# Broadcast rows of the state-space and delta-rule stages: transposes of copied columns instead of products with a triangle

## The chip, the cores and the metric

The kernel runs on 1 core of one Trainium2 chip. The metric is the time of one execution on the device, in microseconds (us); the time given is the median of 3 runs. From the same kernel one profiled execution was taken, and all rows below are from it.

## The reference, cut to what matters

The program is a network of four layers on 512 tokens of width 1024: two layers with a mixer of three branches (attention, spatial gating, a Mamba-2 state space) and two with a gated delta rule, each between feed-forward parts. The change touches two places in it. Both need, for a head, the running sum `cs` of a log decay over the tokens, once as a column (a token on each partition) and once as a row spread over all 128 partitions, to form the decay between token `i` and token `j`:

```python
def segsum(a):                       # state space: a = A * dt, all 4 heads
    cs = jnp.cumsum(a, axis=-1)
    return jnp.where(tril, cs[..., :, None] - cs[..., None, :], -jnp.inf)

# delta rule: chunks of 64 tokens, 4 heads
g = jnp.cumsum(g.reshape(Bsz, N, C, H).transpose(0, 3, 1, 2), axis=-1)
decay = jnp.exp(jnp.where(causal, g[..., :, None] - g[..., None, :], -jnp.inf))
qk = jnp.einsum('bhncd,bhnmd->bhncm', q, k) * decay
q_dec = q * jnp.exp(g)[..., None]
```

The rest of those layers is projections, softmax, normalisations and the recurrences over chunks, which the change leaves as they are.

## The kernel before

T = 512 tokens are TT = 4 tiles of P = 128. The program is a chain of stages; in each, five engines (TensorE, VectorE, ScalarE, GpSimd, SyncE for the DMA queue) run lists of instructions that were written out by hand, in the order in which they stand in the code. Nothing reorders them: an engine that waits for a semaphore holds up all that stands behind it on that engine. A stage ends in a barrier of all engines. `M.ps` is the whole of PSUM, 8 banks of 512 fp32 columns; `M.ident` is the identity, `M.tri` the triangle of ones and `M.ones` a tile of ones.

**mixer1_rest** (twice, for the two layers of the first kind: it starts at 685.9 us and at 1805.0 us) does the state space, the spatial gating and the compressed attention. TensorE begins with `sums_col()`: `A.a` (tokens by tiles and heads) times the triangle gives all 16 running-sum columns in bank 2. Then follow `compress(0)` (32 matmuls, L1696), `turn_ws()` (L1794), `rows(0)`, `turn_x()` (L1801), `rows(1)`, `spatial(0)` and `spatial(1)` (L1770), `states(0, 0)` (L1715), `turn_local(0)` (L1780), `compress(1)`, `turn_local(1)`, `turn_hidden()` (L1807), and later `scores(0)` (L1739), `rows(2)`, `states(0, 2)`, `scores(1)`, `rows(3)`, `turn(0)` (L1750). `rows(h)` makes the spread row of head `h` in bank 4 or 5 (L1704): for each of 4 tiles `j` a matmul whose stationary side is the column `A.a[:, j, h]` spread over 128 columns and whose moving side is the triangle followed by ones, 512, 384, 256 and 128 columns wide, added up in one bank. ScalarE's `decays(g, k)` (L1886, L1887, L1890) reads these banks, with the columns `cs` and `ncs` = -`cs` as bias.

VectorE begins this stage with a memset (L2091), `statistics()` of the spatial gating's layer norm (L2030 to L2033), `bias_columns()` (L2040), then `sums_copy()` (L2044, L2045), which copies the sums from bank 2 to `cs` and `ncs`, then `ws_mask()` (L2049, waits for `turn_ws`), a reciprocal (L2097), four `center(i)` (L2025, L2026, two instructions each), whose last signals `v_normed`, for which `spatial(0)` waits; after them `steps_times_x` (L2055), `gate` (L2016), `low_local(0)` (L170), `weigh(0, 0)` (L1965, L1967), `pre()` (L2060, waits for `compress(1)`; ScalarE then makes `cmp_x`, and `turn_hidden` waits for that). ScalarE begins with a Gelu (L1914), waits for `statistics()`, takes a root (L1916), then six Silu (L1918), one more (L1919), then `decays(0, 0)`.

**mixer2_delta** (twice: from 2413.6 us and from 3121.7 us) does the delta rule. TensorE makes the sums of `A.g` (L2521, L2522) in bank 7. Then for each of 4 token tiles `i`: the spread rows of the 4 heads (L2528, stationary `g` column spread, moving the 128-wide triangle), the rows of beta (L2534, transposes of a spread column), products `kk` (L2536) and `qk` (L2541), transposes of `k` and `v` (L2546, L2551) and `dense(i)`: 24 products of a projection that is done in between (L163 to L165). Before the rows of a tile `i` >= 1 it waits until VectorE has read the previous ones (`S.diff`). After the 4 tiles follow 28 rounds of the triangular inverse (`first_product` L2566 and L2568, `updates` L2577, `turn_inverse` L2586).

VectorE begins this stage with `low(0)` and `low(1)`, the low halves of two weight tiles (L170), each after a cast by ScalarE (L2658); behind them it copies the sums to `A.G` (L2811) and `A.gain` (L2812 to L2814). ScalarE's part in a tile is the Exp of the rows (L2710), the Exp of the differences (L2712), and behind that `evacuate(i)` of the product `dense(i)` (L2673) and the cast of the next weight tile (L2658), which stand ahead of L2710 of the next tile. VectorE's part is L2820, L2821 (differences from the rows), the low halves of the next weights, L2827 to L2842, and in the last tile the first masks of the inverse (`mask`, L2801 and L2805).

Of the kernel before, what the change touches and what calls it, by code (L numbers as in the profile page):

```python
# [22 lines left out]
P = 128  # L23
T = 512
TT = T // P
# [1621 lines left out]
def mixer1_rest(nc, M, A, I, l, mine, ahead):  # L1647
# [7 lines left out]
    with ExitStack() as memory, stage(  # L1655
# [34 lines left out]
        def _(pe):  # L1690
# [9 lines left out]
            def rows(h):  # L1700
                if h >= hpg:
                    pe.wait_ge(S.decay, hpg * TT)
                for j in range(TT):
                    mm = pe.matmul(M.ps[:, 4 + h % 2, j * P:T], A.a[:, j, h:h + 1].to_broadcast([P, P]), tri[:, 0:T - j * P],  # L1704
                                   start=(j == 0), stop=(j == TT - 1), skip_group_check=True)
                mm.then_inc(S.rows, 1)

            def states(g, k):
# [248 lines left out]
        def _(dve):  # L1957
# [131 lines left out]
                low_part(dve, M.h_low[:, n_ssd + g, :], xbc[:, g, :], M.h_high[:, n_ssd + g, :])  # L2089

            dve.memset(bias_c[:], MASKED).then_inc(S.bias_init, 1)  # L2091
            statistics()
            bias_columns()
            sums_copy()
            ws_mask()
            dve.wait_ge(S.root_ready, 1)
            link(dve.reciprocal(rstd[:], rstd[:]))  # L2097
# [360 lines left out]
def mixer2_delta(nc, M, A, I, l, mine, ahead):  # L2458
# [4 lines left out]
    UNITS = TT * LEVELS  # L2463
    sequence = [e for c in range(SCT) for e in ([3 * c, 3 * c + 1, 3 * c + 2] + ([GATED + c - 1] if c else []))] + [GATED + SCT - 1]
    place = {e: n for n, e in enumerate(sequence)}
    with ExitStack() as memory, stage(nc, f"delta_{l}", "sums chain gains gain_exp g_rows diff decay rows_exp q_scaled kk qk "
               "lt_ready qk_ready k_turned v_turned nat_ready masked t1 t1_copied x_up xy_ready y_turned x_copied u_ready w_ready u_copied w_copied "
               "ws state_read v_new o o_squared o_copied o_normed s_add s_ready root_ready prep_free mix_turned mix_high mix_ready sc_high "
               "w_high w_split product act_evacuated dve_evacuated gated squared sc_root sc_scaled pad gate_chain row_high", mine) as (block, S):
# [33 lines left out]
        def _(pe):  # L2503
# [19 lines left out]
            for i in range(TT):  # L2523

                if i >= 1:
                    pe.wait_ge(S.diff, i)
                for h in range(DH):
                    mm = pe.matmul(head(M.ps[:, 0], h), g_all[:, DH * i + h:DH * i + h + 1].to_broadcast([P, P]), tri,  # L2528
                                   start=True, stop=True)
                mm.then_inc(S.g_rows, 1)  # L2530
                if i >= 1:
                    pe.wait_ge(S.lt_ready, i)
                for h in range(DH):
                    pe.transpose(head(M.ps[:, 1], h), beta_all[:, DH * i + h:DH * i + h + 1].to_broadcast([P, P]), M.ident[:])  # L2534
                for h in range(DH):
                    mm = pe.matmul(head(M.ps[:, 2], h), tok(k, h, i), tok(k, h, i), start=True, stop=True)  # L2536
                mm.then_inc(S.kk, 1)
                if i >= 1:
                    pe.wait_ge(S.qk_ready, i)
                for h in range(DH):  # L2540
                    mm = pe.matmul(head(M.ps[:, 3], h), tok(k, h, i), tok(q, h, i), start=True, stop=True)  # L2541
                mm.then_inc(S.qk, 1)
                if i >= 1:
                    pe.wait_ge(S.nat_ready, i)
                for h in range(DH):
                    mm = pe.transpose(head(M.ps[:, 4], h), tok(k, h, i), M.ident[:])  # L2546
                mm.then_inc(S.k_turned, 1)
                if i >= 1:
                    pe.wait_ge(S.prep_free, i)
                for h in range(DH):  # L2550
                    mm = pe.transpose(head(M.ps[:, 5], h), tok(v, h, i), M.ident[:])  # L2551
                mm.then_inc(S.v_turned, 1)
                dense(i)
# [197 lines left out]
        def _(dve):  # L2751
# [56 lines left out]
            gate_link(dve.memset(A.prod[:, :, 0:SCCONV - 1], 0.0))  # L2808
            low(1)
            dve.wait_ge(S.sums, 1)  # L2810
            link(dve.tensor_copy(A.G[:], M.ps[:, 7, 0:16]))  # L2811
            link(dve.tensor_copy(A.gain[:, 0:16], M.ps[:, 7, 0:16]))  # L2812
            link(dve.tensor_tensor(A.gain[:, 16:32], M.ps[:, 7, 16:32], A.G[:], ALU.subtract))
            dve.tensor_copy(A.gain[:, 32:48], M.ps[:, 7, 16:32]).then_inc(S.gains, 1)  # L2814
            dve.wait_ge(S.gain_exp, 1)
# [220 lines left out]
```

## Time and profile before

| | |
|---|---|
| median of 3 runs | 3725.05 us (3722.63 to 3726.55) |
| span of the profiled execution, first to last instruction | 3722.3 us |
| median less that span | 2.7 us |
| TensorE matmul busy | 3579.8 us (96% of the span) |
| VectorE, ScalarE, GpSimd busy | 1981.1, 1221.2, 149.4 us |
| mean granted TensorE clock | 0.979 of full speed |

The profiled execution's own time is its span; what a timed run counts beyond that (launch and end) shows only as the 2.7 us between span and median. PE is TensorE's matmuls, PEld its weight loads, which run ahead under the matmul before; DVE is VectorE, ACT ScalarE. A matmul's duration in the trace contains its modelled way through the array, so two neighbours overlap, and PE looks busy across small waits. How long a group of matmuls holds TensorE is therefore read from the start of its first weight load to the start of the next group's. An fp32 matmul stands as two records, a transpose as one. PEclk is the granted clock: 1.00 is 2.4 GHz and 0.50 is 1.2 GHz.

### The profile page before, as it was taken

The numbers are of one execution on the slowest core, as the hardware profiler recorded it, in microseconds if no ns is written. First come the engines' busy times: TensorE is split into PE (matmuls) and PEld (weight loads), VectorE is DVE, ScalarE is ACT, GpSimd is POOL, SyncE is SP. The second block draws the span as 40 slices with busy tenths as digits, with TensorE's granted clock in tenths as the row PEclk, the third lists the DMA queues.
The fourth block names the chain that finished last, engine by engine and source line by source line (L and its number), as shares of the span: only waits on it lengthen the run. The fifth ranks groups of instructions, "written<-read, shape, count | busy, mean of one in ns | idle before, by whom it ended". The sixth has DMA issues, their size and how long they took to land. (4 is left out here: it accounts for less than half of the span.)

```text
span 3722.3 us, 43542 instructions
## 1 busy us (share of the span) xinstructions
PE 3579.8 (96%) x17858; PEld 2957.7 (79%) x17858; DVE 1981.1 (53%) x3057; ACT 1221.2 (33%) x1920; POOL 149.4 (4%) x212
## 2 busy tenths in 40 slices
PE   6999999999999999999999998999999999999999
PEld 4888778678887888777678886788788878878887
DVE  5555566666456755566663355665322366553233
ACT  2222334432223222334532233634222355342222
POOL 1110100001000110100000001000000000000000
PEclk8999999999999999999999999999999999999999
DMA  6664331145443654331133342211233312113332
GB/s 238 224 200 138 77 94 46 52 132 200 143 136 96 212 173 139 76 97 46 52 122 121 99 145 52 75 39 52 80 102 119 102 47 74 40 52 102 91 107 79
DMA packets 438042, 397.75 MB, mean 107 GB/s; under 512 B 53779, under 2 KB 390275, under 8 KB 437844
## 3 DMA queue, kind: packets, MB, share of 16 engines
q1 hardware_dynamic: 413028, 310.53, 27.5%
q0 software_dynamic: 24816, 84.45, 6.7%
q8 instruction: 141, 2.31, 0.3%
q14 instruction: 57, 0.47, 0.0%
HBM read 390.14 MB, written 4.78 MB: 106 GB/s over the span
## 5 line engine op out<-in xcount | busy, mean ns | idle before, releaser
L163 PE MATMUL m_ps<-m_h_high,ffn_w_high 128*128 128x512 f32 x2100 | 824.1, 392 | 0.8 <-DVE ffn_w_low L170 0.8
L164 PE MATMUL m_ps<-m_h_low,ffn_w_high 128*128 128x512 f32 x2100 | 819.4, 390 | 0.0
L165 PE MATMUL m_ps<-m_h_high,ffn_w_low 128*128 128x512 f32 x2100 | 819.3, 390 | 0.0
L165 PEld LDWEIGHTS m_ps<-m_h_high,ffn_w_low 128*128 128x128 f32 x2100 | 395.5, 188 | 83.7
L163 PEld LDWEIGHTS m_ps<-m_h_high,ffn_w_high 128*128 128x128 f32 x2100 | 396.0, 189 | 83.0 <-issue 0.8
L164 PEld LDWEIGHTS m_ps<-m_h_low,ffn_w_high 128*128 128x128 f32 x2100 | 396.1, 189 | 81.8
L953 ACT ACTIVATE ffn_sil<-m_ps 128x512 f32<-128x512 f32 x132 | 79.0, 599 | 1140.0 <-PE m_ps L165 1140.0
L163 PE MATMUL m_ps<-ffn_w_high,ffn_hid_high 128*128 128x512 f32 x1056 | 411.7, 390 | 0.0
L165 PE MATMUL m_ps<-ffn_w_high,ffn_hid_low 128*128 128x512 f32 x1056 | 411.0, 389 | 0.0
L164 PE MATMUL m_ps<-ffn_w_low,ffn_hid_high 128*128 128x512 f32 x1056 | 410.9, 389 | 0.0
L993 DVE TENSOR_TENSOR ffn_hid<-ffn_sil,m_ps 128x512 f32<-128x512 f32 x110 | 75.5, 687 | 561.3 <-ACT ffn_sil L953 561.3
L170 DVE TENSOR_TENSOR ffn_w_low<-m_raw,ffn_w_high 128x2048 fp32r<-128x2048 f32 (+1 forms) x168 | 303.6, 1822 | 111.6 <-ACT ffn_w_high L947 107.8
L170 DVE TENSOR_TENSOR ffn_w_low<-ffn_rows,ffn_w_high 128x1024 fp32r<-128x1024 f32 x132 | 161.5, 1224 | 292.1 <-ACT ffn_hid_high L961 291.8
L541 ACT CAST ffn_w_high<-ffn_rows 128x1024 fp32r<-128x1024 f32 x132 | 138.5, 1050 | 407.9 <-PE m_ps L165 395.4
L947 ACT CAST ffn_w_high<-m_raw 128x2048 fp32r<-128x2048 f32 x126 | 239.4, 1900 | 0.0
L165 PEld LDWEIGHTS m_ps<-ffn_w_high,ffn_hid_low 128*128 128x128 f32 x1056 | 198.2, 188 | 41.3
L163 PEld LDWEIGHTS m_ps<-ffn_w_high,ffn_hid_high 128*128 128x128 f32 x1056 | 198.2, 188 | 40.9
L164 PEld LDWEIGHTS m_ps<-ffn_w_low,ffn_hid_high 128*128 128x128 f32 x1056 | 198.2, 188 | 40.8
L381 DVE SCALAR_TENSOR_TENSOR ffn_ada_part<-ffn_rows,m_ccol,ffn_ada_part 128x512 f32<-128x512 f32 x224 | 168.1, 751 | 88.2 <-DMA ffn_rows<-in_ada_w 80.1
L367 POOL DMA_DIRECT2D ffn_rows<-in_ada_w x128 | 90.9, 711 | 1533.4 <-issue 939.1
L1490 ACT ACTIVATE attn_probs<-attn_probs,attn_shift 128x128 f32<-128x128 f32 (+3 forms) x128 | 71.0, 555 | 193.6 <-DVE attn_shift L1545 193.6
L163 PE MATMUL m_ps<-m_h_high,proj_w_high 128*128 128x512 f32 (+2 forms) x312 | 130.9, 420 | 1.8 <-DVE proj_w_low L170 1.8
(479 smaller groups left out, 5564.0 us busy)
## 6 DMA issues: line engine op xcount, KB each, us to landing
m_raw<-in_ffn_w SPq DMA_DIRECT2D x176, 512.0 KB, 4.7
ffn_rows<-in_ada_w POOLq DMA_DIRECT2D x128, 512.0 KB, 5.0
ffn_rows<-in_ffn_w SPq DMA_DIRECT2D x88, 512.0 KB, 3.5
m_raw<-in_w_in SPq DMA_DIRECT2D x32, 1024.0 KB, 5.3
m_raw<-in_ffn_w_gate SPq DMA_DIRECT2D x44, 512.0 KB, 3.8
m_raw<-in_ffn_w_up SPq DMA_DIRECT2D x44, 512.0 KB, 4.8
ffn_rows<-in_ffn_w_down SPq DMA_DIRECT2D x44, 512.0 KB, 3.3
m_raw<-in_w_out SPq DMA_DIRECT2D x24, 512.0 KB, 4.6
```

The source lines that it names most:

```text
L163: pe.matmul(out, sh, mh, start=first, stop=False, skip_group_check=True)
L164: pe.matmul(out, sh, ml, start=False, stop=False, skip_group_check=True)
L165: return pe.matmul(out, sl, mh, start=False, stop=last, skip_group_check=True)
L170: return dve.tensor_tensor(low, value, high.bitcast(F32), ALU.subtract)
L367: queue.dma_start(self.slots[:, n % 2], src).then_inc([S.ada0_landed, S.ada1_landed][n % 2], 16)
L381: dve.scalar_tensor_tensor(out=part, in0=self.slots[:, n % 2, j, :], scalar=self.M.ccol[:, k + j:k + j + 1], in1=part, op0=ALU.mult, op1=A ...
L541: return act.copy(self.high[f % self.SLOTS], self.raw[f % self.raws])
L947: act.copy(w_high[:, f % 2], M.raw[:, f % 2]).then_inc(S.wide_high, 1)
L953: act.activation(sil[:, f % 2, :], M.ps[:, 2 * (f % 2), :], ACT.Silu).then_inc(S.silu_done, 1)
L993: dve.tensor_tensor(hid[:, f, :], sil[:, f % 2, :], M.ps[:, 2 * (f % 2) + 1, :], ALU.mult).then_inc(S.hidden_done, 1)
L1490: ins = act.activation(probs(m, g), probs(m, g), ACT.Exp, bias=shift[:, m % 4, g:g + 1], accum_out=sums[:, p % 4, g, b:b + 1])
```

## The change

In `mixer1_rest`, `rows(h)` no longer multiplies by the triangle. It transposes, for each tile, the copied running-sum column `cs` spread over 128 columns, 128 columns wide, 4 in all. The first two heads now wait for the copy (`S.col_copied`), and VectorE's `sums_copy()` stands ahead of `statistics()`. In `mixer2_delta` the 4 rows of a tile are transposes of the copied columns `A.G`; the first tile waits for a new semaphore `g_copied`, which the copy to `A.G` signals, and VectorE waits for it itself before it reads `A.G`.

```diff
--- before.py
+++ after.py
@@ -1700,9 +1700,10 @@
             def rows(h):
                 if h >= hpg:
                     pe.wait_ge(S.decay, hpg * TT)
-                for j in range(TT):
-                    mm = pe.matmul(M.ps[:, 4 + h % 2, j * P:T], A.a[:, j, h:h + 1].to_broadcast([P, P]), tri[:, 0:T - j * P],
-                                   start=(j == 0), stop=(j == TT - 1), skip_group_check=True)
+                else:
+                    pe.wait_ge(S.col_copied, 1)
+                for i in range(TT):
+                    mm = pe.transpose(M.ps[:, 4 + h % 2, tokens(i)], cs[:, SH * i + h:SH * i + h + 1].to_broadcast([P, P]), M.ident[:])
                 mm.then_inc(S.rows, 1)
 
             def states(g, k):
@@ -2089,9 +2090,9 @@
                 low_part(dve, M.h_low[:, n_ssd + g, :], xbc[:, g, :], M.h_high[:, n_ssd + g, :])
 
             dve.memset(bias_c[:], MASKED).then_inc(S.bias_init, 1)
+            sums_copy()
             statistics()
             bias_columns()
-            sums_copy()
             ws_mask()
             dve.wait_ge(S.root_ready, 1)
             link(dve.reciprocal(rstd[:], rstd[:]))
@@ -2463,7 +2464,7 @@
     UNITS = TT * LEVELS
     sequence = [e for c in range(SCT) for e in ([3 * c, 3 * c + 1, 3 * c + 2] + ([GATED + c - 1] if c else []))] + [GATED + SCT - 1]
     place = {e: n for n, e in enumerate(sequence)}
-    with ExitStack() as memory, stage(nc, f"delta_{l}", "sums chain gains gain_exp g_rows diff decay rows_exp q_scaled kk qk "
+    with ExitStack() as memory, stage(nc, f"delta_{l}", "sums chain g_copied gains gain_exp g_rows diff decay rows_exp q_scaled kk qk "
                "lt_ready qk_ready k_turned v_turned nat_ready masked t1 t1_copied x_up xy_ready y_turned x_copied u_ready w_ready u_copied w_copied "
                "ws state_read v_new o o_squared o_copied o_normed s_add s_ready root_ready prep_free mix_turned mix_high mix_ready sc_high "
                "w_high w_split product act_evacuated dve_evacuated gated squared sc_root sc_scaled pad gate_chain row_high", mine) as (block, S):
@@ -2524,9 +2525,10 @@
 
                 if i >= 1:
                     pe.wait_ge(S.diff, i)
+                else:
+                    pe.wait_ge(S.g_copied, 1)
                 for h in range(DH):
-                    mm = pe.matmul(head(M.ps[:, 0], h), g_all[:, DH * i + h:DH * i + h + 1].to_broadcast([P, P]), tri,
-                                   start=True, stop=True)
+                    mm = pe.transpose(head(M.ps[:, 0], h), A.G[:, DH * i + h:DH * i + h + 1].to_broadcast([P, P]), M.ident[:])
                 mm.then_inc(S.g_rows, 1)
                 if i >= 1:
                     pe.wait_ge(S.lt_ready, i)
@@ -2808,8 +2810,9 @@
             gate_link(dve.memset(A.prod[:, :, 0:SCCONV - 1], 0.0))
             low(1)
             dve.wait_ge(S.sums, 1)
-            link(dve.tensor_copy(A.G[:], M.ps[:, 7, 0:16]))
+            dve.tensor_copy(A.G[:], M.ps[:, 7, 0:16]).then_inc(S.g_copied, 1)
             link(dve.tensor_copy(A.gain[:, 0:16], M.ps[:, 7, 0:16]))
+            dve.wait_ge(S.g_copied, 1)
             link(dve.tensor_tensor(A.gain[:, 16:32], M.ps[:, 7, 16:32], A.G[:], ALU.subtract))
             dve.tensor_copy(A.gain[:, 32:48], M.ps[:, 7, 16:32]).then_inc(S.gains, 1)
             dve.wait_ge(S.gain_exp, 1)
```

How the instructions stand now, at the three places where an engine waits or is waited for. First TensorE in `mixer1_rest`, from `turn_ws` on, before (`m_tri` moving with `a_a` stationary are the old rows):

```order
L1794 MATMUL m_ps<-m_ident,a_ws 128x128 x4
L1704 MATMUL m_ps<-m_tri,a_a 128x512
L1704 MATMUL m_ps<-m_tri,a_a 128x384
L1704 MATMUL m_ps<-m_tri,a_a 128x256
L1704 MATMUL m_ps<-m_tri,a_a 128x128
L1801 MATMUL m_ps<-m_ident,a_raw 128x128 x8
```

and the same stretch, to `states(0, 0)`, with the change (`rest_cs` is the copied column; `rows` is now L1706):

```order
L1795 MATMUL m_ps<-m_ident,a_ws 128x128 x4
L1706 MATMUL m_ps<-m_ident,rest_cs 128x128 x4
L1802 MATMUL m_ps<-m_ident,a_raw 128x128 x8
L1706 MATMUL m_ps<-m_ident,rest_cs 128x128 x4
L1771 MATMUL m_ps<-a_uv,rest_wsT 128x256 x4
L1716 MATMUL m_ps<-a_raw 128x512
```

Four matmuls of 1280 columns in all have become four transposes of 512 columns in all, at the same place. Next VectorE at the start of that stage with the change (before, the two rows of `rest_cs` and `rest_ncs` stood just ahead of `rest_wsT`):

```order
L2092 MEMSET rest_bias_c 128x992
L2045 COPY rest_cs<-m_ps 128x16
L2046 TENSOR_SCALAR rest_ncs<-m_ps 128x16
L2031 BN_STATS rest_stats<-a_uv 128x6 x4
L2033 BN_AGGR rest_mv<-rest_stats 128x2 x4
L2034 TENSOR_SCALAR rest_rstd<-rest_mv 128x4
```

The copy, with its wait for `sums_col`, now stands ahead of the statistics, for which ScalarE waits. Last, TensorE at the start of `mixer2_delta` with the change:

```order
L2522 MATMUL m_ps<-b_g,m_tri 128x16
L2523 MATMUL m_ps<-b_g,m_ones 128x16
L2531 MATMUL m_ps<-m_ident,b_G 128x128 x4
L2536 MATMUL m_ps<-m_ident,b_beta 128x128 x4
L2538 MATMUL m_ps<-b_qkv 128x128 x4
```

and VectorE at the same start:

```order
L170 TENSOR_TENSOR delta_w_low<-m_raw,delta_w_high 128x1024
L2810 MEMSET b_prod 128x2x2
L170 TENSOR_TENSOR delta_w_low<-m_raw,delta_w_high 128x1024
L2813 COPY b_G<-m_ps 128x16
L2814 COPY b_gain<-m_ps 128x16
L2816 TENSOR_TENSOR b_gain<-m_ps,b_G 128x16
```

No instruction has moved in this stage: but L2531 on TensorE, which stood third and waited for nothing of VectorE's, now waits for L2813, which stands behind both L170.

## Rows read from the trace of the kernel before

**Rows 1.** Timeline of the weight loads, first mixer1_rest: start, duration, instruction, idle time before.

```profile
694.15 0.30 PEld L1704 LDWEIGHTS m_ps<-m_tri,a_a 128*128 128x128 f32 x2
...
696.31 0.91 PEld L1801 LDWEIGHTS m_ps<-m_ident,a_raw 128*128 128x128 f32 x8
697.18 0.30 PEld L1704 LDWEIGHTS m_ps<-m_tri,a_a 128*128 128x128 f32 x2
...
699.34 1.60 PEld L1770 LDWEIGHTS m_ps<-a_uv,rest_wsT 128*128 128x128 f32 x8
...
706.17 0.42 PEld L1780 LDWEIGHTS m_ps<-m_ident,a_uv 128*128 128x128 f32 x4 [0.39 <-issue]
```

**Rows 2.** Timeline of VectorE in the same stretch.

```profile
694.46 0.69 DVE L2049 TENSOR_TENSOR rest_wsT<-m_ps,m_tri 128x512 f32<-128x512 f32 x1 [3.23 <-PE m_ps L1794]
...
698.54 0.48 DVE L2026 SCALAR_TENSOR_TENSOR a_uv<-a_uv,rest_rstd,a_ln_b 128x256 f32<-128x256 f32 x1
...
706.53 0.42 DVE L2060 TENSOR_TENSOR rest_cmp_x<-m_ps,a_cmp_b 128x256 f32<-128x256 f32 x1
```

**Rows 3.** Timeline at the starts of both mixer1_rest stages.

```profile
686.15 1.42 PE L1788 MATMUL m_ps<-a_a,m_ones 128*128 128x12 f32 x6
686.95 1.75 DVE L2030 BATCH_NORM_STATS2 rest_stats<-a_uv 128x6 f32<-128x256 f32 x4
...
1805.21 1.01 PE L1788 MATMUL m_ps<-a_a,m_ones 128*128 128x12 f32 x6
1806.04 1.75 DVE L2030 BATCH_NORM_STATS2 rest_stats<-a_uv 128x6 f32<-128x256 f32 x4
```

**Rows 4.** Timeline of ScalarE: its waits for the rows, first stage, then second.

```profile
696.66 1.28 ACT L1886 ACT_TABLE_LOAD   x1 [0.61 <-PE m_ps L1704]
...
699.65 0.58 ACT L1886 ACTIVATE rest_decay<-m_ps,rest_ncs 128x384 f32<-128x384 f32 x1 [0.86 <-PE m_ps L1704]
...
1817.18 0.58 ACT L1886 ACTIVATE rest_decay<-m_ps,rest_ncs 128x384 f32<-128x384 f32 x1
```

**Rows 5.** Timeline around rows(2), rows(3) and turn(0), first stage.

```profile
714.29 0.42 DVE L1990 TENSOR_TENSOR rest_score_c<-rest_score_c,rest_denom_c 128x248 f32<-128x248 f32 x1
...
717.45 0.88 PEld L1750 LDWEIGHTS m_ps<-m_ident,rest_score_c 128*31 128x31 f32 x8
```

**Rows 6.** Timeline of the weight loads at the start of the first mixer2_delta.

```profile
2413.59 0.30 PEld L2521 LDWEIGHTS m_ps<-b_g,m_tri 128*128 128x128 f32 x2 [1.36 <-issue]
...
2414.03 0.97 PEld L2528 LDWEIGHTS m_ps<-m_tri,b_g 128*128 128x128 f32 x8
...
2414.92 0.47 PEld L2534 LDWEIGHTS m_ps<-m_ident,b_beta 128*128 128x128 f32 x4
2415.36 0.97 PEld L2536 LDWEIGHTS m_ps<-b_qkv 128*128 128x128 f32 x8
...
2418.02 0.19 PEld L163 LDWEIGHTS m_ps<-m_h_high,delta_w_high 128*128 128x128 f32 x1
```

**Rows 7.** Timeline of VectorE there: the copy to A.G.

```profile
2417.10 0.17 DVE L2811 COPY b_G<-m_ps 128x16 f32<-128x16 f32 x1
```

**Rows 8.** Timeline of ScalarE and VectorE in and behind the last tile, first mixer2_delta.

```profile
2443.24 1.05 ACT L2658 CAST delta_w_high<-m_raw 128x1024 fp32r<-128x1024 f32 x1
2444.18 0.60 ACT L2710 ACTIVATE b_rows<-m_ps 128x512 f32<-128x512 f32 x1
...
2444.81 0.69 DVE L2820 TENSOR_TENSOR b_D<-m_ps,b_G 128x512 f32<-128x512 f32 x1 [2.44 <-ACT b_rows L2710]
...
2467.29 0.68 DVE L2801 TENSOR_TENSOR b_D<-b_LT,m_levels 128x512 f32<-128x512 f32 x1
```

**Rows 9.** Windows: stretch, its length, busy time by engine, PEclk, DMA share, GB/s.

```profile
682.70:686.10 3.40, 1.57 (x15) 1.46 (x15) 2.02 (x11) 1.29 (x3) 0.00 (x0) 1.00 0.02 5
686.10:692.90 6.80, 6.80 (x34) 4.51 (x35) 4.68 (x16) 5.19 (x7) 0.00 (x0) 0.50 0.00 0
...
1805.70:1809.10 3.40, 3.40 (x17) 2.15 (x19) 3.09 (x12) 1.82 (x3) 0.00 (x0) 0.50 0.00 0
```

## The prediction, as it stands on record

> **What bounds the kernel now.** I read the timeline of TensorE's weight loads first, from the start of one group to the start of the next, because the modelled ends of matmuls hide its waits; then what VectorE and ScalarE do in the same stretches; then the granted clock in windows. The reader is to see that TensorE is nearly always at work and the other engines mostly wait for it, but that this does not hold where the change is made. In `mixer1_rest` VectorE ends its last `center` at 698.54 + 0.48 = 699.02 us [rows 2], and TensorE begins `spatial(0)`, which waits for that, at 699.34 [rows 1]: 0.3 us apart, so two engines arrive together. At the start of `mixer2_delta` TensorE works from 2413.59 on without a gap [rows 6], and the copy to `A.G` is made only at 2417.10 [rows 7], since it is behind two casts' low parts; so far nobody waits for it but ScalarE. And both stages begin with a pause at the barrier, after which the clock can be at half.
>
> **The change part by part.**
>
> *The price of rows.* Old `rows(h)`: 696.31 - 694.15 = 2.16 us. Eight transposes of the same width took 697.18 - 696.31 = 0.87 us, 0.109 each [rows 1]; four transposes of a spread column, just what the new rows are, 2415.36 - 2414.92 = 0.44 us against 2414.92 - 2414.03 = 0.89 for the four products of a delta tile [rows 6]. So a `rows(h)` gives back 1.72 us and a delta tile 0.45. By count TensorE loses 8 x 1.72 + 8 x 0.45 = 17.4 us of work; what follows is how much of it ends up on the path. The lower end of the new price is this 0.44, the upper that of the products of equal width, 0.89.
>
> The Trainium skill, page "TensorE: Matmul & The Clock Gate", section "Part 4: PE-mode transpose", puts a full transpose at about 275 ns inside a kernel. This trace shows 109 ns, so it does not agree; by the page's figure the 64 transposes would cost an estimated 64 x 0.166 = 10.6 us more than by the row.
>
> *First half of mixer1_rest (rows(0), rows(1)).* `turn_ws` is not moved, and the copy is long there, so the new wait costs nothing. TensorE is through with both rows 2 x 1.72 = 3.44 us earlier, at 695.90. But `ws_mask` starts behind `turn_ws` at 694.46 and `center` ends at 699.02 whatever TensorE does [rows 2]: `spatial(0)` starts at 699.06 in place of 699.34. TensorE stands 3.16 us. From there to `turn_local(1)` it needs 706.17 - 699.34 = 6.83 us [rows 1], to 705.9, and VectorE's `pre()` was at 706.53 [rows 2], on ScalarE's chain. ScalarE waited 0.61 + 0.86 = 1.47 us for the rows in the first stage and not at all in the second [rows 4]. Against it stands the moved copy: VectorE now waits for the sums, which end at 686.15 + 1.42 = 687.57, then copies (some 0.3 us), so the statistics start at 687.9 in place of 686.95, 0.95 later; in the second stage 1805.21 + 1.01 + 0.34 = 1806.56 in place of 1806.04, 0.5 later [rows 3]. ScalarE's Silu and decays are queued behind them. Net at `turn_hidden`: 0.5 us gained in the first stage, 0.5 lost in the second, 0 in sum, if the clock holds.
>
> *The clock in that pause.* With TensorE busy 1.57 us of 3.40, the granted clock fell from 1.00 to 0.50, and stayed for 6.8 us in the first stage and 3.4 us in the second [rows 9]. That is 2.4 to 1.2 GHz. The new pause is 3.16 us with only transposes ahead of it. I expect one half-clock stretch of 3.4 us behind it, 1.7 us of work lost: TensorE is then at 699.06 + 6.83 + 1.7 = 707.6, 1.1 behind the old `pre()`. Ends: 0 and 1.1 + 1.7 = 2.8 per stage. The same page's section "Why this matters for your kernels" warns of idle gaps between bursts, after which the clock is back at half; by that rule, the trace agrees (0.50 behind the pause).
>
> *Second half (rows(2), rows(3)).* 3.44 us less work, but `turn(0)` waits for L1990, which ends at 714.29 + 0.42 = 714.71, and TensorE, 3.44 before 717.45, would be there at 714.01 [rows 5]. Gain 717.45 - 714.75 = 2.7; VectorE's chain behind (the next probabilities and `weigh(0, 3)`) takes, as I choose, 0.3 of it: 2.4. TensorE has less dense work here too, so another half-clock stretch is about as likely as not; it would cost 1.5, I count 0.7. Per stage 1.1 - 2.4 + 0.7 = -0.6, both -1.2 us.
>
> *Start of mixer2_delta.* The rows of tile 0 now wait for `A.G`: 2417.10 + 0.17 = 2417.27 [rows 7], TensorE goes on at 2417.31, 3.28 us after 2414.03. All that is queued behind waits too: beta's rows, `kk`, `qk`, two transposes, `dense(0)`. The latter came 2418.02 - 2414.92 = 3.10 us after the old rows' end; now 2417.31 + 0.44 + 3.10 = 2420.85, which is 2.83 late [rows 6]. ScalarE's evacuation and its cast of the next weights wait for `dense(0)`, so nothing absorbs it. Tiles 1 and 2 give back 0.45 each: 1.93 late at the end of `dense(2)`. Tile 3's 0.45 does not count: ScalarE does the cast at 2443.24 and L2710 right behind it at 2444.18, VectorE's L2820 waits for that, and then VectorE has no gap until 2467.29 [rows 8], while TensorE waits for its masks. If it did count, 1.5. I take 1.9 per stage.
>
> *The clock there.* From 1.36 us ahead of 2413.59 [rows 6] to 2417.31 TensorE does only 0.44 us of work. That is emptier than the stretch of 1.57 in 3.40 [rows 9], so half clock when it resumes is nearly sure; the end is open: 1.4 us lost where the stretch began just before, 3.4 where it lasts 6.8 as in the first `mixer1_rest`. I take 2.2. Both stages: 2 x (1.9 + 2.2) = +8.2 us.
>
> **Sum.** -1.2 + 8.2 = +7.0 us: 3722.3 + 7.0 = 3729.3 for the span; the median of the runs stood 2.7 above the span, so 3725.05 + 7.0 = 3732.05, say 3732.
>
> **The rivals.**
> - *The clock holds everywhere.* Then 0 - 2 x 2.4 + 2 x 1.9 = -1.0: 3724.1. Against it are [rows 9].
> - *Half clock lasts.* 3.4 us in each delta start and both stretches in each rest stage: 2 x (1.9 + 3.4) + 2 x (1.1 - 2.4 + 1.5) = +11.0: 3736. For it speaks the 6.8 us stretch. The page's "Part 4" says that transposes do not bring the full clock on as matmuls do, which would come out the same way; by the rows, the transposes at 696.31 ran at 0.109.
> - *Faster: TensorE's work is the path in mixer1_rest after all.* That needs v_normed not to bind, decided at L1770: if it starts before 696 us, both halves count, 4 x 3.44 = 13.8 less, and with the stall of 3.8 it is -10: 3715. Against it is VectorE's end at 699.02.
> - *A transpose of a copied column costs as much as a product* (0.89 for four): the delta stages save nothing, 2 x (3.3 + 2.2) = +11, the rest stages about 0: 3736.
>
> **How the numbers follow.** This kernel's runs lie within 4 us, so 0.2%, 7.5 us, is about what a measurement can tell. My own case has 58 in 100, with a range of +2 to +11; it straddles that bound, 24 above and 34 below. The clock holds: 14. Half clock lasts: 15. Dear transposes: 3. Faster: 10. So faster 0.10, within 0.2% 0.34 + 0.14 = 0.48, slower 0.24 + 0.15 + 0.03 = 0.42. The range goes from 3723, under the case of the held clock, to 3738, above the two slow ones.
>
> **What would show it.** L2531 starting near 3.3 us after L2523, behind L2813; the windows at both delta starts at 0.50; four new rows in 0.44 us at full clock; L1771 no more than 0.3 us earlier against the stage's start, with TensorE idle ahead of it; L2031 later by 0.95 and 0.5; `mixer1_rest` shorter by 0 to 3 us, `mixer2_delta` longer by 2 to 5. I would be wrong if `dense(0)` did not come later, if the clock stayed at 1.00 in those windows, or if half-clock stretches elsewhere moved by several.

## The result and the profile after

The kernel with the change takes 3743.05 us (median, 3729.66 to 3753.79), the kernel before 3725.05 us in the same session: 18.0 us more, ratio 1.0047 with a 95% interval of 1.0037 to 1.0056. I had forecast 3732, in a range of 3723 to 3738. Slower by over 0.2% had 0.42 of my chances; the size is outside the range.

The page of the kernel after, its span and the busy time of each engine:

```profile
span 3727.8 us, 43426 instructions
...
PE 3569.4 (96%) x17794; PEld 2950.2 (79%) x17794; DVE 1979.8 (53%) x3057; ACT 1221.4 (33%) x1920; POOL 149.5 (4%) x212
```

Against before, TensorE has 10.4 us less busy time, and still the kernel is slower. Note that this profiled execution is the quickest of all that were timed; a second profiled one is nearer to the median. The cores view of that second one:

```profile
core 0: 3746.6 us, clock 0.971
```

So I read places from the traces and the size of an effect from the timed runs. The mean granted clock stands beside the span of each timed run, and it splits the loss in two. The clock shows two levels only, 1.00 and 0.50, so 2 x (1 - clock) x span is the time spent at half. Over the runs of the kernel after that is 211 us, over those of the kernel before in the four sessions of the experiments 155 to 162 us. Span times clock, the work as if done at full clock, is 3635.5, against 3644.9 for the kernel before in the first of these sessions (156 at half). The change takes 9 us of work away and brings some 55.6 us of half clock, half of which is lost: 27.8 - 9.4 = 18.4. This is bookkeeping, and it comes out for any kernel: it says how much half clock there is, not where it lies or what brings it.

**First mixer1_rest.** Timeline of the weight loads, the same columns as [rows 1]:

```profile
694.87 0.46 PEld L1706 LDWEIGHTS m_ps<-m_ident,rest_cs 128*128 128x128 f32 x4
695.31 0.91 PEld L1802 LDWEIGHTS m_ps<-m_ident,a_raw 128*128 128x128 f32 x8
696.18 0.46 PEld L1706 LDWEIGHTS m_ps<-m_ident,rest_cs 128*128 128x128 f32 x4
699.87 2.23 PEld L1771 LDWEIGHTS m_ps<-a_uv,rest_wsT 128*128 128x128 f32 x8 [3.22 <-DVE a_uv L2027]
702.19 0.76 PEld L1716 LDWEIGHTS m_ps<-a_raw 128*128 128x128 f32 x2
...
709.43 0.20 PEld L1808 LDWEIGHTS m_ps<-m_ident,rest_cmp_x 128*128 128x128 f32 x2 [0.63 <-ACT rest_cmp_x L1928]
...
715.51 0.41 PEld L1706 LDWEIGHTS m_ps<-m_ident,rest_cs 128*128 128x128 f32 x4
716.75 0.79 PEld L1751 LDWEIGHTS m_ps<-m_ident,rest_score_c 128*31 128x31 f32 x8 [0.83 <-DVE rest_score_c L1991]
```

`rows(0)` holds TensorE 695.31 - 694.87 = 0.44 us; TensorE then stands 3.22 us for `v_normed`; behind that pause it is at half clock (L1771 to L1716 is 2.32 us, before it was 1.63). `turn(0)` comes 716.75 - 709.43 = 7.32 us behind `turn_hidden`, before 717.45 - 707.44 = 10.01.

**VectorE at that start**, as in [rows 2, 3]:

```profile
688.05 0.17 DVE L2045 COPY rest_cs<-m_ps 128x16 f32<-128x16 f32 x1 [0.31 <-PE m_ps L1789]
...
688.22 1.80 DVE L2031 BATCH_NORM_STATS2 rest_stats<-a_uv 128x6 f32<-128x256 f32 x4
...
699.33 0.48 DVE L2027 SCALAR_TENSOR_TENSOR a_uv<-a_uv,rest_rstd,a_ln_b 128x256 f32<-128x256 f32 x1
```

No long stretch of half clock stands behind `turn(0)` in this execution: its two `mixer1_rest` stages took 62.99 and 62.07 us, before 65.26 and 62.84. (Such lengths are read from the first load of the sums to the first load of the output projection.) In the second profiled execution of the same kernel the second stage took 71.65 us, with 37.5 us at half where the first execution had 16.8; that stage is 9.6 of the 18.8 us between the two spans.

**Start of mixer2_delta**, weight loads as in [rows 6], the last row being `dense(0)`:

```profile
2421.02 0.30 PEld L2522 LDWEIGHTS m_ps<-b_g,m_tri 128*128 128x128 f32 x2 [1.35 <-issue]
2421.24 0.30 PEld L2523 LDWEIGHTS m_ps<-b_g,m_ones 128*128 128x128 f32 x2
2424.75 0.71 PEld L2531 LDWEIGHTS m_ps<-m_ident,b_G 128*128 128x128 f32 x4 [3.20 <-DVE b_G L2813]
2425.45 0.87 PEld L2536 LDWEIGHTS m_ps<-m_ident,b_beta 128*128 128x128 f32 x4
...
2429.73 0.19 PEld L163 LDWEIGHTS m_ps<-m_h_high,delta_w_high 128*128 128x128 f32 x1
```

The wait for L2813 is there as forecast, 3.51 us from L2523 to L2531 (forecast 3.3), and `dense(0)` starts 8.71 us after L2522, before 4.43. Two windows, in front of and behind the wait's end (busy time of PE, PEld, DVE, ACT, POOL; PEclk; DMA share; GB/s):

```profile
2419.00:2422.40 3.40, 1.46 (x12) 1.19 (x10) 1.41 (x5) 2.04 (x4) 0.00 (x0) 1.00 0.00 0
2424.50:2427.90 3.40, 3.15 (x15) 3.15 (x16) 2.07 (x8) 0.84 (x2) 0.00 (x0) 0.50 1.01 253
```

### The profile page after: what moved, and what is told of

Its sections match the earlier page's. It is cut to its first block and busy times, and to the rows that moved or that the text cites. A ratio compares the mean times of both kernels' runs of the same rounds, so it can differ in the third digit from the quotient of the medians.

```text
span 3727.8 us, 43426 instructions
## 1 busy us (share of the span) xinstructions
PE 3569.4 (96%) x17794; PEld 2950.2 (79%) x17794; DVE 1979.8 (53%) x3057; ACT 1221.4 (33%) x1920; POOL 149.5 (4%) x212
## 5 line engine op out<-in xcount | busy, mean ns | idle before, releaser
L170 DVE TENSOR_TENSOR ffn_w_low<-m_raw,ffn_w_high 128x2048 fp32r<-128x2048 f32 (+1 forms) x168 | 303.6, 1822 | 112.1 <-ACT ffn_w_high L947 108.5
L170 DVE TENSOR_TENSOR ffn_w_low<-ffn_rows,ffn_w_high 128x1024 fp32r<-128x1024 f32 x132 | 161.5, 1223 | 291.6 <-ACT ffn_hid_high L961 291.5
```

Of the source, the lines that this page charges most:

```text
L170: return dve.tensor_tensor(low, value, high.bitcast(F32), ALU.subtract)
```

## The experiments

Two theories stood at first. **A**: the loss is half-clock time, set off where a wait or the shortened rows leave TensorE with too little to do. **B**: it is the waits themselves, the late `dense(0)` and the late statistics. Unless said otherwise a kernel is timed against the kernel before on its own chip; those medians were 3725.42, 3721.48, 3726.27 and 3725.74 us in the four sessions below. "More than before" is the difference of the two medians; the ratio, with its interval, is worked out from all runs and can differ from it by some 2 us, so where the two disagree the ratio is the better guide. "At half" is the mean over its runs of the time at half clock, worked out as above.

### One part alone, one stall removed, and the change again

`rest_only` has the edit of `mixer1_rest` alone, `delta_only` that of `mixer2_delta` alone. `reorder` has both, with the rows of tile 0 behind the transposes of `k` and `v` (shortened; "spread rows" stands for the four transposes and their signal):

```diff
-                else:
-                    pe.wait_ge(S.g_copied, 1)
-                spread rows of tile i
+                if i >= 1:
+                    spread rows of tile i
...
                 mm.then_inc(S.v_turned, 1)
+                if i == 0:
+                    pe.wait_ge(S.g_copied, 1)
+                    spread rows of tile 0
                 dense(i)
```

Expected of `rest_only`:

> Only mixer1_rest changed, mixer2_delta as before. Theory A (the loss is the wait at the start of mixer2_delta and the half clock behind it): 0 to -4 us against before, mixer1_rest stages 1 to 2 us shorter, one new half-clock stretch in each. Rival B (the thinner TensorE work in mixer1_rest lets the clock fall so often that it is the main loss): +6 to +12 us. Rival C (the new half-clock time lies in stages that the change does not touch, by chance of where the clock looks): about 0 with a wide spread.

Of `delta_only`:

> Only mixer2_delta changed, mixer1_rest as before. Theory A: most of the 18 us of the change, +12 to +18, with dense(0) 2.8 us later and half clock behind the wait in both stages. Rival B: +4 to +8, the stalls alone with one half-clock stretch each. Rival C: about +4.

Of `reorder`:

> The whole change, but in mixer2_delta the rows of tile 0 stand behind the transposes of k and v, 3.10 us later in TensorE's order, so that the wait for the copy to A.G ends at about the time TensorE gets there. Theory A: the wait and the half clock behind it vanish, dense(0) is 0.4 us earlier than before the change, and the time is that of the rest-only kernel less 2 us. Rival B: still +5 or more over before, all of it in mixer1_rest.

Of the changed kernel once more:

> The changed kernel once more, for its time beside the others on one chip and for a second trace. All theories: +14 to +21 us over before. Its trace tells how far half-clock time in stages that the change does not touch differs from one execution to the next: rival C expects such stages to differ by 5 us or more between this trace and the first.

| kernel | median, us | more than before | ratio, 95% interval | at half, before's |
|---|---|---|---|---|
| rest_only | 3742.31 | +16.9 | 1.0046 (1.0028 to 1.0064) | 211, 156 |
| delta_only | 3732.65 | +7.2 | 1.0023 (1.0010 to 1.0036) | 174, 156 |
| reorder | 3736.39 | +11.0 | 1.0028 (1.0014 to 1.0042) | 203, 156 |
| after_again | 3745.73 | +20.3 | 1.0057 (1.0037 to 1.0076) | 215, 156 |

The delta part costs about what I had forecast for it (7.2 us against 8.2). The part that I had at -1.2 costs 17 here. Part of it shows in the windows of the second `mixer1_rest`, four stretches of 6 us that begin near `rows(2)` (this stage starts 2.2 us earlier in `rest_only`). The kernel before:

```profile
1828.00:1834.00 6.00, 6.00 (x37) 4.30 (x36) 5.21 (x16) 1.25 (x3) 0.00 (x0) 1.00 1.04 249
1834.00:1840.00 6.00, 6.00 (x39) 3.97 (x38) 2.95 (x8) 4.71 (x18) 0.00 (x0) 0.98 0.28 66
1840.00:1846.00 6.00, 6.00 (x34) 4.13 (x36) 4.48 (x14) 1.79 (x7) 0.00 (x0) 0.73 0.02 4
1846.00:1852.00 6.00, 5.54 (x39) 3.29 (x35) 4.65 (x10) 1.26 (x3) 0.00 (x0) 1.00 0.00 0
```

and `rest_only`:

```profile
1828.00:1834.00 6.00, 5.41 (x38) 4.65 (x38) 5.18 (x17) 3.31 (x10) 0.00 (x0) 0.73 0.76 186
1834.00:1840.00 6.00, 6.00 (x20) 2.82 (x21) 2.55 (x6) 2.96 (x12) 0.00 (x0) 0.50 0.00 1
1840.00:1846.00 6.00, 6.00 (x28) 4.69 (x29) 3.62 (x11) 1.51 (x5) 0.00 (x0) 0.50 0.00 0
1846.00:1852.00 6.00, 6.00 (x26) 2.93 (x22) 0.93 (x3) 0.00 (x0) 0.00 (x0) 0.57 0.01 3
```

Read the counts beside PEclk: 20 matmuls where there were 39. PE is "busy" for the full 6 us in both, so its share says nothing here. The half clock starts with `turn(0)`, as the weight loads of `rest_only` show:

```profile
1830.66 1.43 PEld L1751 LDWEIGHTS m_ps<-m_ident,rest_score_c 128*31 128x31 f32 x8 [0.83 <-DVE rest_score_c L1991]
...
1832.90 2.66 PEld L1740 LDWEIGHTS m_ps<-rest_kcT,a_qT 64*128 64x128 f32 x16 [0.22 <-issue]
```

The gain of the short rows is there, TensorE waits 0.83 us for L1991, and from then on `scores` takes 2.66 us for its 16 loads where it takes 1.44 at full clock. But the same short rows and the same wait don't always bring it. The second stage of the changed kernel, first execution, keeps the full clock:

```profile
1834.02 0.79 PEld L1751 LDWEIGHTS m_ps<-m_ident,rest_score_c 128*31 128x31 f32 x8 [0.82 <-DVE rest_score_c L1991]
...
1835.42 1.44 PEld L1740 LDWEIGHTS m_ps<-rest_kcT,a_qT 64*128 64x128 f32 x16
```

In the second stage of `reorder` a long stretch begins 1.8 us ahead of `turn(0)`, which does not wait there at all. So the wait for L1991 is neither needed for it nor enough.

Rival C of these expectations, half clock in stages that the change does not touch: between the two executions of the changed kernel no such stretch of the program differs by over 2.6 us; between kernels one does, as told under "What stays open".

`reorder` does what it should at the delta start: its loads run on and the copy is ready when it is asked for, 0.21 us short:

```profile
2427.91 0.30 PEld L2523 LDWEIGHTS m_ps<-b_g,m_ones 128*128 128x128 f32 x2
2428.05 0.50 PEld L2537 LDWEIGHTS m_ps<-m_ident,b_beta 128*128 128x128 f32 x4
...
2430.74 0.47 PEld L2554 LDWEIGHTS m_ps<-m_ident,b_qkv 128*128 128x128 f32 x4
2431.42 0.41 PEld L2528 LDWEIGHTS m_ps<-m_ident,b_G 128*128 128x128 f32 x4 [0.21 <-DVE b_G L2817]
```

Its two delta stages, from the first load of the sums to the first of the output projection, are 175.13 and 173.47 us; `delta_only` has 180.99 and 180.40, the kernel before 174.75 and 176.50.

### Half of the rest edit, padding, and the stall without its clock

`rest_first` transposes for heads 0 and 1 only (with the moved copy), `rest_second` for heads 2 and 3 only (copy at its old place). `rest_pad` is `rest_only` with work put back (shortened):

```diff
+                if h >= hpg:
+                    for _ in range(2):
+                        pe.matmul(M.ps[:, 4 + h % 2, :], M.ident[:], M.tri[:, 0:T], start=True, stop=True)
                 for i in range(TT):
                     mm = pe.transpose(...)
```

`delta_fill` is `delta_only` with three such products (bank 6) ahead of the wait for `g_copied`.

> mixer1_rest alone, and of it only the first half: rows of heads 0 and 1 as transposes with the moved sums_copy, rows of heads 2 and 3 as products as before, delta rule as before. Theory A (the loss of rest_only, +17 us, is half-clock time set off where rows(2) and rows(3) became short just before the wait of turn(0)): this kernel is within 3 us of the kernel before, its second mixer1_rest is near 62 us and shows no half-clock stretch of 13 us or more that starts before turn(0). Rival B (the moved sums_copy and the pause of TensorE behind rows(0), rows(1) set it off, and it only shows later): this kernel carries the loss, +12 to +17 us, and its second mixer1_rest is at 68 us or more. Rival C (each half takes its share): +6 to +9 us.

> The other half of the same edit: rows of heads 0 and 1 as products with sums_copy where it was, rows of heads 2 and 3 as transposes, delta rule as before. Theory A: carries most of the loss, +10 to +17 us, with a half-clock stretch of over 13 us that starts at turn(0) of the second mixer1_rest (stage at 68 us or more). Rival B: within 3 us of the kernel before. Rival C: +6 to +9 us.

> rest_only with two useless fp32 products of 512 columns (identity by triangle, into the bank that the rows then fill) ahead of rows(2) and of rows(3), so that TensorE has work there again for about 1.8 us each, and the transposes stay. Theory A (the short rows leave TensorE too little to do before turn(0), and the clock falls): the long half-clock stretch of the second mixer1_rest is gone, its stage is at 62 to 64 us, and the kernel is within 4 us of the kernel before, although it has more work than rest_only. Rival B (the first half sets it off): the loss stays at +12 us or more, with up to 7 us of padding on top of it. Rival D (transposes themselves, not their shortness, count as little work for the clock): the stretch stays too.

> The delta rule's change alone (mixer1_rest as before), with three useless fp32 products of 512 columns into a free bank while TensorE stands before the wait for the copy of A.G: the wait and all that it delays stay, but TensorE is busy in it. Theory A (of delta_only's +6.2 and +3.9 us in the two stages, the stall is about 2 each and the rest half clock): stages at about 176.7 and 178.4 us, whole kernel +3 to +5. Rival E (the late start of k and v transposes and of dense(0) costs it all, clock or no clock): stages stay at about 181 and 180.4 us, whole kernel +7 to +10. If the products run past the wait they add their overrun to both.

| kernel | median, us | more than before | ratio, 95% interval | at half, before's |
|---|---|---|---|---|
| rest_first | 3727.88 | +6.4 | 1.0011 (0.9997 to 1.0024) | 170, 155 |
| rest_second | 3723.88 | +2.4 | 1.0005 (0.9993 to 1.0017) | 178, 155 |
| rest_pad | 3729.73 | +8.3 | 1.0015 (1.0003 to 1.0026) | 173, 155 |
| delta_fill | 3727.15 | +5.7 | 1.0014 (1.0004 to 1.0024) | 159, 155 |

Theory A's picture holds and its number fails. `rest_second` has the half clock behind `turn(0)`, as `rest_only` has; here the same first two windows:

```profile
1828.00:1834.00 6.00, 5.41 (x35) 4.71 (x34) 4.83 (x15) 3.96 (x13) 0.00 (x0) 0.68 0.80 187
1834.00:1840.00 6.00, 6.00 (x16) 2.89 (x16) 2.91 (x7) 1.83 (x10) 0.00 (x0) 0.50 0.00 1
```

but it costs 2.4 us in all, and not 10 to 17; `rest_first` has no such stretch, but its second stage takes 66.62 us where I expected 62. Neither half alone can be told from the kernel before (both intervals contain 1), so neither carries the +16.9; whether both together cost more than their sum of 9 is a question to which the repeat of `rest_only` below belongs. `rest_pad`, which has both halves and some 7 us more work, has less half clock than `rest_only` and is quicker, and its windows behind the padding are at full clock:

```profile
1828.00:1834.00 6.00, 6.00 (x42) 4.04 (x40) 4.97 (x15) 2.08 (x4) 0.00 (x0) 1.00 0.91 242
1834.00:1840.00 6.00, 6.00 (x49) 4.83 (x49) 4.04 (x13) 2.57 (x9) 0.00 (x0) 1.00 0.74 180
1840.00:1846.00 6.00, 6.00 (x39) 3.52 (x40) 4.60 (x12) 4.28 (x17) 0.00 (x0) 1.00 0.01 4
```

Its padding also brings TensorE to `turn(0)` late enough not to wait there. Not all came as expected: its second stage takes 66.61 us, with a long stretch later in it, where I had 62 to 64, so in the traces its two stages together (132.3 us) are no shorter than those of `rest_only` (131.8), which do without the padding.

`delta_fill` parts stall and clock. Weight loads of `delta_only`, then of `delta_fill`:

```profile
2422.85 0.30 PEld L2521 LDWEIGHTS m_ps<-b_g,m_tri 128*128 128x128 f32 x2 [1.35 <-issue]
...
2426.58 0.71 PEld L2530 LDWEIGHTS m_ps<-m_ident,b_G 128*128 128x128 f32 x4 [3.21 <-DVE b_G L2812]
...
2432.81 0.19 PEld L163 LDWEIGHTS m_ps<-m_h_high,delta_w_high 128*128 128x128 f32 x1
```

```profile
2419.50 0.30 PEld L2521 LDWEIGHTS m_ps<-b_g,m_tri 128*128 128x128 f32 x2 [1.35 <-issue]
...
2423.22 0.41 PEld L2532 LDWEIGHTS m_ps<-m_ident,b_G 128*128 128x128 f32 x4 [1.27 <-DVE b_G L2814]
...
2426.70 0.19 PEld L163 LDWEIGHTS m_ps<-m_h_high,delta_w_high 128*128 128x128 f32 x1
```

The wait ends equally late, 3.73 and 3.72 us after the stage's first load. With TensorE busy in it, `dense(0)` comes 7.20 us after that load; with TensorE idle 9.96; in the kernel before 4.43. So the stall delays it by 2.77 and the clock by another 2.76. The stages were 178.25 (with a half-clock stretch at 2477 that the kernel before has not) and 176.62 us.

### A second trace of before, the first pause filled, and the better order

`rest_fill` is `rest_only` with three of those products (bank 2) between `rows(1)` and `spatial(0)`. `delta_reorder` is the kernel before with the delta edit in the order of `reorder`, and `second_reorder` adds the transposes of heads 2 and 3 to it.

> The kernel before once more, for a second trace. In the first one the second mixer1_rest took 62.84 us with 10.2 us of half clock and the stretch from its output projection to the first delta stage 545.78 with 23.9. Theory A (the long half-clock stretch behind turn(0) comes from the short rows): again no stretch of 13 us or more there, the stage within 3 us of 62.8. Rival F (it is a matter of where the clock's looks fall, and the first trace was a lucky one): a long stretch or a stage at 66 us or more here too. Time 3712 to 3735 by either.

> rest_only with three useless fp32 products of 512 columns (2.7 us at full clock) between rows(1) and spatial(0), where TensorE stood about 3 us; the second half keeps its short rows. The two halves apart cost +6 and +2 us by the medians, together +17. If the pause of the first half is what brings the surplus (it costs a half-clock stretch of its own, and leaves less work ahead of the second half's gap): +1 to +6 us, with the half-clock time of all runs, 2 x (1 - clock) x span, back from about 211 to about 180 us. If the surplus comes from the second half alone or from the moved sums_copy: +12 us or more, half-clock time above 200. The long stretch behind turn(0) of the second mixer1_rest stays in either case.

> The delta rule's change alone, with the rows of tile 0 behind the transposes of keys and values, mixer1_rest as before. The order takes the stall away (in the reordered whole change the two stages were at +0.4 and -3.0 us), so the stages should be at 175 and 173.5 to 176.4 us, and the kernel at 0 to -3 us against the kernel before. If the delta_only loss of +7 came not from the stall but from the short rows of tiles 1 to 3, it stays at +5 or more.

> The candidate for the best version: transposes for heads 2 and 3 alone in mixer1_rest, and the delta rule as in delta_reorder. If the parts add up: +2 (rest_second) and -2 to 0 (delta_reorder), so 0 to +2 us, no gain that can be told. If the half-clock stretches of the parts add to more than their sum, as the two halves of mixer1_rest do: +5 or more. Faster than before by over 7 us only if the long stretch behind turn(0) shows in few of the runs.

| kernel | median, us | more than before | ratio, 95% interval | at half, before's |
|---|---|---|---|---|
| before_again | 3728.83 | +2.6 | 1.0009 (0.9997 to 1.0020) | 167, 162 |
| rest_fill | 3729.75 | +3.5 | 1.0015 (1.0004 to 1.0027) | 187, 162 |
| delta_reorder | 3724.53 | -1.7 | 0.9994 (0.9982 to 1.0006) | 169, 162 |
| second_reorder | 3721.60 | -4.7 | 0.9994 (0.9982 to 1.0006) | 175, 162 |

The unchanged kernel differs from itself by 2.6 us, so less than that is nothing. Its second trace has the second `mixer1_rest` at 62.83 us, no long stretch: against rival F. `rest_fill` is at +3.5 where `rest_only` was at +16.9, while its own stretch behind `turn(0)` stays (windows two and three at 0.50):

```profile
1834.00:1840.00 6.00, 6.00 (x27) 4.12 (x24) 2.54 (x8) 3.89 (x14) 0.00 (x0) 0.50 0.24 59
1840.00:1846.00 6.00, 6.00 (x19) 3.31 (x19) 3.64 (x9) 1.51 (x5) 0.00 (x0) 0.50 0.00 1
```

That points to the pause of the first half as a part of the loss. The order of `delta_reorder` takes away the loss of `delta_only`. `second_reorder` has the lowest median of all, though its trace has the long stretch behind `turn(0)` in both stages (68.85 us each); neither of the two can be told from the kernel before.

### Short, or transposes?

`rest_pad` could not tell whether the clock falls because the rows are short or because they are transposes. So the same time was filled with transposes (shortened):

```diff
-                    for _ in range(2):
-                        pe.matmul(M.ps[:, 4 + h % 2, :], M.ident[:], M.tri[:, 0:T], start=True, stop=True)
+                    for n in range(16):
+                        pe.transpose(M.ps[:, 4 + h % 2, tokens(n % TT)], M.tri[:, 0:P], M.ident[:])
```

> rest_pad with the padding made of transposes: sixteen useless transposes of 128 x 128 (16 x 0.109 = 1.74 us) ahead of rows(2) and of rows(3), in place of the two products (1.76 us), so that TensorE is occupied for the same time in the same places. If what keeps the clock is that TensorE is occupied, this is like rest_pad: +4 to +10 us, half-clock time of all runs near 173 us, no long half-clock stretch behind turn(0) of the second mixer1_rest. If transposes do not count for the clock as products do: like rest_only or worse, +15 to +25 us, half-clock time at 200 us or more, the stretch there.

> The kernel of rest_only again, on the chip of rest_pad_turned and for a second trace: +14 to +20 us, with a half-clock stretch of over 13 us in one of its two mixer1_rest stages (7 of the 14 such stages traced so far had one). If it comes out at +10 us or less, the first number was partly its chip's or its hour's.

`rest_pad_turned`: 3729.26 us, +3.5, ratio 1.0010 (1.0000 to 1.0021), 173 us at half. `rest_only_2`: 3735.68 us, +9.9, ratio 1.0030 (1.0017 to 1.0043), 203 us at half. With transposes as padding (1.70 us from the first row to the second of its weight loads) the clock stays at 1.00, as the windows behind them show:

```profile
1831.47 1.73 PEld L1707 LDWEIGHTS m_ps<-m_ident,m_tri 128*128 128x128 f32 x16
1833.17 0.47 PEld L1709 LDWEIGHTS m_ps<-m_ident,rest_cs 128*128 128x128 f32 x4
```

```profile
1834.00:1840.00 6.00, 6.00 (x60) 5.60 (x58) 4.00 (x15) 2.59 (x8) 0.00 (x0) 1.00 0.85 195
1840.00:1846.00 6.00, 6.00 (x43) 3.81 (x43) 4.64 (x12) 4.67 (x18) 0.00 (x0) 1.00 0.00 1
```

So it is the shortness of the rows, or the wait that it leaves, and not the kind of instruction: with either padding 173 us are at half. Part 4 of the Trainium skill's page "TensorE: Matmul & The Clock Gate" has it that transposes do not count as busy for the clock in the way of matmuls; these windows, in which the transposes stand among other matmuls, do not show it. This pair is also the cleanest comparison of all, since both were timed in one session: the padded kernel is 6.4 us quicker by the medians than the same kernel without its useless work.

The repeat corrects the first number: the rest edit alone costs 10 to 17 us, not 17, and the two intervals overlap. With it, two readings from above become weaker. The halves' sum of 9 is not clearly less than the whole. And `rest_fill` is clear only of the first `rest_only` (1.0004 to 1.0027 against 1.0028 to 1.0064), not of the second (1.0017 to 1.0043).

## Why the prediction was wrong, point by point

- **The price of rows: right.** 0.44 us for four transposes in `mixer1_rest`, 0.109 each; in tiles 1 to 3 of `mixer2_delta` 0.55 where the products took 1.00, so the 0.45 of the forecast. The rival of dear transposes is out. One comparison in the prediction was wrong, without touching the sum: 0.109 us is the distance from one transpose to the next, and one transpose's own record is far longer, since neighbours overlap:

```profile
L1706 PE MATMUL m_ps<-m_ident,rest_cs x32: 272/273/323, 695.0 to 1833.2; 128*128 128x128 f32 x32
```

The about 275 ns that Part 4 of the Trainium skill's page "TensorE: Matmul & The Clock Gate" gives are such a duration. The trace agrees with it (median 273 ns), and the estimate of 10.6 us more was worked out from the wrong one of the two.
- **The pause ahead of spatial(0): right.** Forecast 3.16 us, measured 3.22, behind VectorE's L2027. The moved copy made the statistics 0.56 and 0.24 us later against the stage's start, where I had 0.95 and 0.5. The half clock behind the pause lasted 3.4 us in both stages, as forecast, and `turn_hidden` came 1.28 and 0.89 us later, forecast 1.1. The rival "faster" had its condition in L1770 starting before 696 us; TensorE still waited for VectorE.
- **turn(0) earlier: right at full clock.** Forecast 2.4 to 2.7, measured 10.01 - 7.32 = 2.69.
- **The delta start: right in kind, somewhat short in size.** The stall was forecast as 2.83 us at `dense(0)` and 1.9 per stage; measured 2.77, and 176.62 - 174.75 = 1.9 (the second stage of `delta_fill` against the first of the kernel before, each with 1 us at half; the second trace of before has 174.80 and 174.72). The clock was forecast at 2.2 per stage; it took 2.76 by `dense(0)`, and 2.7 and 3.8 over the whole stages (180.99 - 178.25, 180.40 - 176.62). Whole: 7.2 us against 8.2.
- **The step that failed** is the last of the second half of `mixer1_rest`: "another half-clock stretch is about as likely as not; it would cost 1.5, I count 0.7". The likelihood was right and the size was not. Over all traces there are 16 such stages in which `rows(2)` and `rows(3)` are short and unpadded (eight traces, two stages each); in 9 of them half clock of 13.7 to 20.5 us begins within 2 us of `turn(0)`, and these nine take 69.7 us in the mean, the other seven 62.7. Not 1.5 but 7 us: the nine have 33.1 us at half in the mean, the seven 18.2, and half of that difference is 7.5. In the 16 stages in which these rows are long or padded, none has it, and none is over 66.7 us. I had taken the length of a stretch from [rows 9], 3.4 and 6.8 us. The trace of before held a longer one in this very stage, 23 us behind `turn(0)`, and I passed it over:

```profile
740.70:754.40 13.70, 12.04 (x51) 9.58 (x51) 7.42 (x14) 3.63 (x7) 0.00 (x0) 0.50 0.16 43
```

By the nine of sixteen the term should have been 3.9 us and not 0.7, some 3 more per stage. That is at most some 6 of the 11 us by which the forecast of 3732 fell short. The rest is loss that I had at nothing, outside the places that I had priced, and where it comes from stays open (below).
- **Sums of terms.** I added the stretches as if each were its own. The two halves, +6.4 and +2.4 us apart, make +10 to +17 together. That hints at more than a sum, but the intervals do not show it. What I wrote as a sign of being wrong, half-clock stretches that move elsewhere by several us, is what came.
- **The rival "half clock lasts"** (+11, 3736) was nearest in kind, with the same flaw: it counted 1.5 for the second stretch. Dear transposes gave the same 3736 with a mechanism that did not come.
- **The spread.** I took 4 us, the spread of three runs; the 17 runs of the kernel before that were timed beside the changed one reach from 3715.92 to 3736.74.

**What stays open.** The mean of the 16 stages, 66.6 us, is 2.0 above that of the ten unchanged ones (64.6), so the traces place some 4 of the 10 to 17 us there. The others may lie in stages that the change does not touch: from the second output projection to the first delta stage the two traces of before take 545.8 and 545.7 us, with 23.9 at half; all those with the whole rest edit except `rest_fill` 552.5 to 553.7, with 34 to 37 at half. But `rest_first` and `delta_reorder` have 552.9 and 552.7 there too and lose little, and `rest_fill` 549.5. In `delta_only`, `delta_fill` and `delta_reorder` the program up to there is that of the kernel before, and they took 549.7, 549.7 and 552.7, so 7 us there come without any change, and I can't assign it. How the first pause adds to the loss was not found either. It does not show in how often the long stretch comes: 5 of 10 stages with the pause, 4 of 6 with the pause filled or never made. Each trace is one execution.

## What to carry to other kernels

Where TensorE is near the path and other engines' results end its waits, a shorter instruction group is no gain in itself: ask whether the time comes back as a pause, and what work follows the pause. How long a stretch of half clock lasts varied in `mixer1_rest` from 3.4 to 20.5 us. The long ones at `turn(0)` have small matmuls and short waits behind them, and those of [rows 9] mostly dense products; that this is what decides the length is my reading, not shown by a run, and the same place was at half for 13.7 us in one execution of the kernel before and for 3.4 in the other. So read the price at the place itself, from more than one trace, and never carry it over from another place. And when a copy gets a new reader on another engine, place the reader behind work that doesn't need it (-1.7 against +7.2 us for the delta part here) before judging the change.

## What the runs showed of the hardware that I had not expected

- Useless work made a kernel quicker: `rest_pad_turned`, with 16 transposes more ahead of each of two groups of rows per stage, took 3729.26 us where `rest_only_2` took 3735.68 in the same session; at half 173 us against 203. `rest_fill` points the same way (+3.5 us, 187 at half).
- Transposes as padding hold the granted clock at 1.00 as products do (173 us at half in both padded kernels).
- The granted clock moves this kernel's time even unchanged: two traces of the kernel before, 3722.3 and 3716.9 us, differ in the first `mixer1_rest` alone by 65.26 - 62.87 = 2.4 us, with 17.2 and 10.2 us at half. Two of the changed kernel differ in the second by 71.65 - 62.07 = 9.6 us, with 37.5 and 16.8.
